# Attention units of two query tiles alternate, and everything that follows a unit moves one slot later

## What is computed

```python
def stick_breaking_attend(q, k, v, q_pos, k_pos):       # 8 heads of 64
    z = einsum('bqhd,blhd->bhql', q, k) / sqrt(HEAD_DIM)
    log_keep = where(mask, log_sigmoid(-z), 0.0)
    log_rest = cumsum(log_keep, axis=3, reverse=True) - log_keep
    a = where(mask, exp(log_sigmoid(z) + log_rest), 0.0)
    return einsum('bhql,blhd->bqhd', a, v)

def nsa_compressed_selected(...)   # 8 query heads: softmax over 31 compressed blocks, and over the selected blocks
def window_attend(...)             # the same heads, softmax over the window
def merge_nsa_branches(o_cmp, o_sel, o_win, gates)      # gated sum of the three

def finish_layer(x, o_sb, o_nsa, ...):
    mix = concatenate([rms_norm(o_sb, g1), rms_norm(o_nsa, g2)])
    x = x + mix @ w_out                                 # 1024 x 1024
    h = rms_norm(x, norm_ffn)
    return x + hierarchical_moe(h, ...)                 # 1 of 4 groups, then 2 of its 4 experts
```

## Time and profile before

| | us |
|---|---|
| median of 3 runs | 852.58 (852.19 to 853.59) |
| the profiled execution | 852.32 |
| its span, first to last instruction | 850.5 |
| slots 0 to 47 with what is turned and multiplied after them | 273.5 to 515.0 |
| last output products and routing | 515.0 to 547.2 |
| experts, final norm | 547.2 to 850.5 |

### The profile page before, as it was taken

The page is one execution under the profiler, slowest core; times in us unless marked ns, Lnnn a source line. Parts: engine busy times, 40 slices in busy tenths (PEclk is TensorE's granted clock), DMA queues, the critical chain, the costliest instruction groups (busy, mean ns, idle before and its releaser), DMA issues.

```text
span 850.5 us, 12084 instructions
## 1 busy us (share of the span) xinstructions
PE 749.5 (88%) x4522; PEld 399.0 (47%) x4522; DVE 387.7 (46%) x884; ACT 219.9 (26%) x561; POOL 57.2 (7%) x87
## 2 busy tenths in 40 slices
PE   5976999967998687887888889589999999999987
PEld 2454455525645333534444555334545456544532
DVE  5421014473201665777767774537332443222245
ACT  1221101112201344556466652100111111110113
POOL 0121000200000000010000000210000000000040
PEclk9998999997998555999999999699999999999999
DMA  8136956084237910000000027497899999999982
GB/s 315 41 75 182 316 197 223 14 288 133 87 113 240 311 81 0 3 1 1 27 1 1 26 99 277 118 382 272 292 411 387 412 379 397 408 400 400 413 322 102
DMA packets 95884, 173.20 MB, mean 204 GB/s; under 512 B 20946, under 2 KB 33970, under 8 KB 95794
## 3 DMA queue, kind: packets, MB, share of 16 engines
q1 hardware_dynamic: 84626, 150.75, 49.6%
q10 hardware_dynamic: 7904, 11.37, 3.6%
q0 software_dynamic: 3296, 10.30, 3.5%
HBM read 153.08 MB, written 21.41 MB: 205 GB/s over the span
## 4 chain that ended last, share of the span: by engine, by line
PE 50%; DVE 10%; DMA 6%; issue 6%; ACT 5%; SPq 1%; POOL 0%; ACTq 0%; DVEq 0%
PE bank L2331 15%; PE bank L2761 5%; PE bank L2322 5%; PE bank L1736 4%; PE bank L1663 4%; PE bank L2743 4%; DMA qreg<-w_gate 3%; PE bank L1682 2%; ACT reg L1149 2%; PE bank L2365 2%; DVE st L1309 1%; PE bank L2450 1%; PE bank L2455 1%; DVE reg L1320 1%; DMA work<-h_rows,ids 1%
## 5 line engine op out<-in xcount | busy, mean ns | idle before, releaser
L2761 PE MATMUL bank<-reg 128*128 128x512 f32 (+1 forms) x384 | 167.0, 582 | 1.2 <-DVE reg L2702 0.9
L2331 PE MATMUL bank<-reg,qreg 128*32 128x128 f32 (+2 forms) x880 | 118.3, 373 | 1.2 <-issue 0.8
L2761 PEld LDWEIGHTS bank<-reg 128*128 128x128 f32 x384 | 72.6, 198 | 69.9 <-issue 66.7
L2331 PEld LDWEIGHTS bank<-reg,qreg 128*32 128x32 f32 (+2 forms) x880 | 62.3, 135 | 53.6 <-issue 41.6
L2743 PE MATMUL bank<-cf,reg 128*128 128x128 f32 (+1 forms) x384 | 64.8, 299 | 13.6 <-DVE reg L2693 9.4
L1736 PE MATMUL bank<-reg 128*128 128x512 f32 x128 | 63.3, 606 | 0.0
L2743 PEld LDWEIGHTS bank<-cf,reg 128*128 128x128 f32 (+1 forms) x384 | 45.6, 152 | 34.1 <-issue 29.8
L2618 ACT ACTIVATE work<-bank 128x128 f32<-128x128 f32 (+6 forms) x107 | 41.4, 413 | 69.1 <-PE bank L2743 61.0
L1682 PE MATMUL bank<-work,vreg 128*64 128x128 f32 x480 | 40.8, 302 | 11.3 <-ACT work L2618 10.1
L2702 DVE COPY work<-bank 128x128 f32<-128x128 f32 (+4 forms) x56 | 23.1, 425 | 55.2 <-PE bank L2743 55.1
L2322 PE MATMUL bank<-reg,work 128*128 128x512 f32 x96 | 42.5, 595 | 0.0
(11 more groups left out here) (336 smaller groups left out, 956.0 us busy)
## 6 DMA issues: line engine op xcount, KB each, us to landing
reg<-w_gate SPq DMA_DIRECT2D x12, 2048.0 KB, 19.5
reg<-w_up SPq DMA_DIRECT2D x12, 2048.0 KB, 19.1
reg<-w_down SPq DMA_DIRECT2D x12, 2048.0 KB, 19.9
reg<-w_in SPq DMA_DIRECT2D x4, 2048.0 KB, 8.5
expert_rows<-vreg SPq DMA_DIRECT2D x11, 512.0 KB, 5.2
reg<-cache_sb_k SPq DMA_DIRECT2D x16, 256.0 KB, 4.8
reg<-cache_sb_v SPq DMA_DIRECT2D x16, 256.0 KB, 3.6
qreg<-w_up SPq DMA_DIRECT2D x2, 2048.0 KB, 14.1
```

The source lines that it names most:

```text
L2331: ins = T.matmul(bank[which][rows, at_:at_ + w], rowsT[b][:, k, r0:r0 + n], w_[:, k, h * w:(h + 1) * w], start=(k == 0), stop=(k == KD - 1))
L2761: ins = nc.tensor.matmul(at("m", ("proj", n))[:, 0:w], hT[:, k, i * P:(i + 1) * P], win[:, pos % 2, k, 0:w], start=(k == 0), stop=(k == KD ...
```

## The change

Line numbers of the changed kernel are 9 to 12 higher than those of before in this part (L1663 becomes L1672, L1682 L1691, L1736 L1745, L1123 L1132, L1173 L1182, L2618 L2627, L2743 L2752).

1. The triples no longer go tile by tile. They go 3, 0, 3, 0, 3, 0, 3, 0, 2, 1, 1, 2, 1, 1, 2, 2. Tile 2 is now the last and tile 1 the last but one.
2. Every unit is turned one slot later: SEL and WIN three slots after their score, SB six. `pv`, still one slot behind, and `evac` move with it. The loop has one slot more.
3. `cprobT` has two buffers. The compressed branch of tiles 3, 0, 2, 1 is placed at slots 0 to 2, 3 to 5, 18 to 26, and 27 to 29.
4. The output products stand in fewer slots: 2 in each of 10 to 13 for the samples, 4 in each of 26 to 29 for tile 3 and 30 to 33 for tile 0, and 3, 3, 3, 3, 4 in 47 to 51 for tile 1. The routing starts at slots 14 (samples), 30 (tile 3) and 38 (tile 0), before 16, 28 and 40.
5. The scaling of `w_out` on DVE moves from slots 2, 3, 6, 7 to 4, 5, 7, 8.

```diff
-    cprobT = view(work, 6912, [2, P])
+    cprobT = [view(work, 6912, [2, P]), sb("cprob_turned", [P, 2, P])[:, :, :]]
-    tile_order = [QT] + list(range(QT))
+    TRIPLES = (3, 0, 3, 0, 3, 0, 3, 0, 2, 1, 1, 2, 1, 1, 2, 2)
+    tile_order = [QT, 3, 0, 1, 2]
+    SHARES = {2: 3, 1: 0}
+    HALF = {3: 0, 0: 1, 2: 0, 1: 1}
-        place((2, 3, 6, 7)[q], scale_wout, k)
+        place((4, 5, 7, 8)[q], scale_wout, k)
-        for q, count in enumerate((1,) * 8 if i == QT else (1, 1, 2) * 4):
+        for q, count in enumerate(counts):
-    units = [(i, b, p) for i in range(QT) for p in range(REP) for b in range(3)]
+    units = [(i, b, TRIPLES[:k].count(i)) for k, i in enumerate(TRIPLES) for b in range(3)]
-        t -= 5 if t % 3 == WIN else 2
+        t -= 6 if t % 3 == SB else 3
-    for n, i in enumerate(tile_order[:-1]):
-        place_output(i, 4 + PER_TILE * n)
-    for n, i in enumerate(tile_order[:-2]):
-        place_route(i, 4 + PER_TILE * (n + 1))
+    place_output(QT, 10, (2, 2, 2, 2))
+    place_output(3, 26, (4, 4, 4, 4))
+    place_output(0, 30, (4, 4, 4, 4))
+    place_output(1, 47, (3, 3, 3, 3, 4))
+    place_route(QT, 14)
+    place_route(3, 30)
+    place_route(0, 38)
+    CMP_SLOTS = {0: ("score", 3), 1: ("norm", 3), 2: ("turn", 3), 3: ("score", 0), 4: ("norm", 0), 5: ("turn", 0),
+                 18: ("score", 2), 21: ("norm", 2), 26: ("turn", 2), 27: ("score", 1), 28: ("norm", 1), 29: ("turn", 1)}
-    for t in range(len(units) + 4):
+    for t in range(len(units) + 5):
```

101 lines of the change are left out of this document (51 added, 50 removed).

## The result

The changed kernel takes 882.01 us (median of 4 runs, 880.82 to 884.22) against 852.38 us for the kernel before: ratio 1.036, 95% interval 1.032 to 1.040. The forecast was slower, 862 us, range 843 to 873. The sign was right and the size three times too small: +30, not +10.

The account below looks back on a forecast made before the run. No engine was full; the pace came from a chain through PE, ACT and DVE. The terms -7 + 8 - 5 - 5 + 9 + 8 + 2 = +10 on 852.3 us gave 862 us, range 843 to 873.

Parts of the forecast that it names:

- second buffer: ACT's three waits for the last `pv` of the tile ahead, 7.4 us, go: -7, bounds -7.4 and -4.
- turning later: On ACT, `evac` and two SEL copies come between SEL's exponentials and Relu in tile 0 triples: +8.
- clock: Early attention: clock rises after three triples, not five, leaving two slices at 5 instead of three: -5.
- slots without products: Slots 14 to 25 and 34 to 46, where PE was nearly last, lose their output products: -5.
- crowded slots 26 to 33: 32 products, 48 us of PE work, make PE the bound without idle time, triples 16 us or more: +9.
- behind the last score: From last WIN score to last `pv`, 16 products instead of 7, 24 to 25 us instead of 16.7: +8.
- scaling, squares: Two `w_out` scalings on DVE leave SB slots, squares move to a SEL and a WIN slot: +2.
- the 23 that would have refuted the step: Sign against the forecast: pairs of tiles 3 and 0 under 23 us on average mean the copies were covered.
- After the last `pv`: From last `pv` to the end stays 335.5 us within 2 us; otherwise the prediction is wrong.
- The faster case: Rival: light triples take up the heavy ones' load in attention: -12, 840 us; chance 0.28.
- The much slower case: Rival: the clock stays at 1.2 GHz well into the pairs of tiles 3 and 0: 872 us; chance 0.12.
- the clock's rival: Clock term of the much slower case: low through six triples, +5 instead of -5; chance 0.12.

Follow-up runs that it names:

- c3: b1 with only the last of every four output products of tiles 0, 1 and 2 (36 of 48 left out); first SB score to last `pv` 4.4 us longer.
- b1: Kernel before with the second buffer for turned compressed probabilities, nothing else; ratio 0.9915.
- a1: Changed kernel with turning back at two and five slots, all else as changed; ratio 1.0434.
- b2: b1 with every unit turned one slot later, output products and routing of the prompt tiles with it, old order of tiles; ratio 1.0114.
- b4: b2 with each tile's squares, products and routing two slots further back, so that the squares fall into SB slots; ratio 1.0045.
- b6: b1 with 5 matmuls that nobody reads added in PE's waits of slots 1 to 3; ratio 0.9845.
- a7: Changed kernel without 16 of the 32 output products in slots 26 to 33; first SB score to last `pv` 263.6 us against 274.0.
- b3: Kernel before with the 16 output products of tiles 0, 1 and 2 as four in each of four slots; ratio 1.0348, 878.55 us.
- a3: Changed kernel with last triples 2, 1, 1, 1, 1, 2, 2, 2 and tile 1's products two a slot in slots 44 to 51; ratio 1.0296.
- c1: Changed kernel with the scaling of `w_out` back in slots 2, 3, 6 and 7; ratio 1.0376.
- a5: a1 with each tile's squares in an SB slot (24, 27, 45) and products starting one slot earlier; ratio 1.0341.
- c2: a6 with only the last of every four output products of tiles 3, 0 and 1 (36 of 48 left out); first SB score to last `pv` 2.9 us from c3.
- a6: a5 with the last triples ordered as in a3, tile 1's squares in slot 42 and its products two in each of slots 43 to 50; ratio 1.0221.

## Why the prediction was right and wrong

The forecast was 20 us short, and the steps that failed are those on the output products. The sum took their absence from slots 14 to 25 and 34 to 46 as a gain of 5; c3 shows none, but 4.4 us of loss, in the old order. It put +9 on the 32 products in slots 26 to 33, from 48 us of PE work with PE never idle; the three triples that hold them took 60.2 us, PE busy 54.2. And it put +8 on the end, where +18 was measured. The later turn, +8 in the sum, failed the other way and hid part of the miss. By the steps of the sum, in us:

| step | predicted | shown by | measured |
|---|---|---|---|
| second buffer | -7 | b1 | -7.2 |
| turning later | +8 | a1, b2 with b4 | new order: -6 (-11 to -2) by the ratios, +1.5 in the traces of attention; old order: -1 before the last score and +9 behind it, in the traces |
| clock | -5 | windows, b6 | rises early, falls again; no gain |
| slots without products | -5 | c3 against b1 | no gain, rather +4 |
| crowded slots 26 to 33 | +9 | a7, b3, window | 0.71 per product; +21 if the chain is the 39 that the sum took, which was not measured |
| behind the last score | +8 | window, a3 | +18 |
| scaling, squares | +2 | c1, a5 | 0 and up to +8 (4 in the traces), part of it at the end, so also in the row above |

**The second buffer** was sized right. The wait of ACT's copy for L1697 is gone.

**Turning later** is a step whose mechanism failed. The rows were as predicted: in the first triple of tile 0 Relu starts at 297.59, 2.15 us behind the exponentials of SEL, with the two copies and the large `sb_exp` between. But the light triples were not bound by ACT. In the four of them PE is busy 84, 98, 88 and 92% and ACT 49 to 58%. The fourth triple, of the changed kernel:

```profile
318.84:333.01 14.17, 13.89 (x134) 8.67 (x135) 6.75 (x23) 6.93 (x20) 0.00 (x0) 0.74 0.00 1
```

PE does the turns and `pv` of the heavy unit there at a clock of 0.74. I had taken the chain as the bound there because it was the bound in the old order. That the pairs took 28.3, 30.1, 31.9 and 27.7 us, far over the 23 that would have refuted the step, was no proof of it: they were long for another reason.

**The clock.** The rise came earlier than the three triples that I had given it: in the second (0.84 over it; 0.65 and 0.66 in a3 and a7), so the row has no 5 where I had asked for two. What I left out is that it could fall again. The sum took the products as a load that PE would be glad to lose in slots 14 to 25 and 34 to 46; c3 shows the opposite. I used them as -5 in one term, and priced the clock only up to its first rise in another, so no term asked what the emptied slots do to the clock.

**The crowded slots.** The mechanism held in the last two of the three triples (PE busy 18.37 of 19.30 us and 18.40 of 18.40, where I had asked for 16 or more with no idle time). Its size didn't: the three triples that hold slots 26 to 33 take 60.2 us. I had compared 48 us of PE work with a chain of 39. It is 54.2 us of PE work, 6 more, and 6.0 of idle time. The first of the three has 5.0 of that idle time and products at the lower clock besides, so neither bound alone gives its 22.5 us.

```profile
392.55:415.05 22.50, 17.46 (x84) 9.06 (x83) 11.83 (x23) 9.18 (x24) 0.00 (x0) 0.85 0.00 1
...
434.35:452.75 18.40, 18.40 (x114) 10.09 (x113) 10.58 (x24) 8.02 (x23) 0.00 (x0) 1.00 0.07 30
```

**Behind the last score** three things make the +18. The count was off: I set 16 products against 7, but two of the seven stand behind the last `pv` (L1736 at 514.93, against 513.90 for the `pv`), so it is 11 more, 9.5 us at 0.86, not 7.7. The squares were the larger miss: I had seen them go from SB slots to "a SEL and a WIN slot" and put +2 on all of it. With them come PE's wait of 4.35 (in which the squares are 1.08 on ACT and their sums 1.92 on DVE; the rest is the chain behind them), the sums of 1.0, and the lower clock, which costs some 2.9 of the 5.47 us (six instructions are 2.6 at 0.43). And DVE empties the one `x` bank inside two slots, 0.84 us of waiting each, which I had named without a price. Together 19.5, less the 0.5 for smaller `pv` and turns and the 1.2 that PE was idle there before: 17.8 against the 18.1 measured.

**After the last `pv`** I expected 335.5 us within 2; it took 332.3, 2.7 of the difference in last products and routing (29.45 us against 32.2 in the earlier trace rows). By my own sign that is outside what I allowed. No experiment is about it, and the same stretch took 330.0 to 334.3 us in b1, b2, b4, a1 and a5, so one trace of each kernel doesn't show that the change did it.

**The rivals.** The faster case rested on light triples taking up the heavy ones' load. The Trainium skill, "Perfetto Trace Analysis", section "Optimization Strategy", holds that stretches with different busiest engines may gain by interleaving. c2 against c3 shows no gain here, but +2.9 us, in agreement with the remark that tiles 0 and 3 don't differ much in that. The much slower case had the right suspect, the clock, in the wrong form: not low for long at the start, but low again and again. The outer sums contain a slip: the bounds as listed, with the +5 of the clock's rival, give 832 and 895, not 831 and 887.

The ratios give a way from the kernel before to the changed one: to b1 -7, b1 to a6 +26 (alternation with the crowding it forces), a6 to a5 +10 (the order at the end), a5 to a1 +8 (squares and one slot), a1 to the changed kernel -6, together +31. The steps share their kernels, so they add up whatever they are worth; each is known to 4 to 6 us either way.

**Left open.** Whether the later turn helps as a whole in the new order: its -6 by the ratios has no counterpart in attention. What it does in the first eight triples is better shown: 117.95, 120.37 and 120.26 us with it (changed kernel, a3, a7) against 122.25, 124.58, 124.62 and 121.51 without (a1, a5, a6, c2), some 4 us less; how much of that is the clock isn't known. How a5's 8 us divide between the squares and the slot isn't known either.

## What to carry to other kernels

Small independent work that lies in an engine's waits can be worth more than nothing: gathering it elsewhere costs most of its length there (0.71 of 0.86 us each), and the place it leaves may slow down. Before moving a step that occurs once a tile, look which slot kind it lands in; 1.08 us on ACT and 1.91 on DVE ahead of a reduction that everyone waits for became 7.5 us in one triple of b2 and 3.5 and 3.8 in two others. And when a sum has one term for a stretch at low clock, ask in the same line what keeps the clock up afterwards.

## What was not expected of the hardware

- PE can be busy by the profile and its clock stay at 1.2 GHz: 12.40 of 12.70 us at 0.50 in b1. The Trainium skill, "TensorE: Matmul & The Clock Gate", section "What's actually happening", says that the activity of PE releases the throttle; here, with five matmuls of 128 rows by 512 columns ahead of it, the same work ran at 1.00 (b6), and without them it did not.
- 36 output products fewer, 4.4 us more (c3 against b1, one trace of each).
- The same plan gives different times by when the clock rises: the first eight triples, equal in the changed kernel, a3 and a7, took 117.95, 120.37 and 120.26 us. Differences of 2 us between single profiles are therefore no evidence.
